# Three of the MLP's four parts of up units in pairs of seven block products, with the input sums made behind the first eight units

## The reference

```python
def sqrelu_mlp(x, w1, w2):        # x 512x1024, w1 1024x4096, w2 4096x1024
    h = jax.nn.relu(x @ w1)
    return (h * h) @ w2

for layer in range(2):
    mix = hybrid_mixer(...) if layer == 0 else recurrent_mixer(...)
    x = layer_norm(DN_ALPHA * x + mix, ...)
    x = layer_norm(DN_ALPHA * x + sqrelu_mlp(x, mlp_w1[layer], mlp_w2[layer]), ...)
```

## Time and profile before

| what | value |
|---|---|
| median of 3 runs | 2314.28 us (2313.63 to 2316.79) |
| the profiled execution's own time | 2314.27 us |
| its span, first to last instruction | 2312.2 us |
| PE busy | 2289.0 us, 99% |
| PE weight load busy | 1954.3 us, 85% |
| DVE busy | 1481.2 us, 64% |
| ACT busy | 1110.8 us, 48% |
| POOL busy | 340.1 us, 15% |
| granted TensorE clock, mean | 1.000 |

### The profile page before, as it was taken

How to read it: one execution, slowest core, us unless ns; L and a number is a source line. 1 busy time by engine, 2 the same in 40 slices (tenths; PEclk the granted TensorE clock), 3 DMA queues, 4 the chain that set the end, 5 groups by cost and what they waited for, 6 DMA issues and landing times.

```text
span 2312.2 us, 33438 instructions
## 1 busy us (share of the span) xinstructions
PE 2289.0 (99%) x13578; PEld 1954.3 (85%) x13578; DVE 1481.2 (64%) x2282; ACT 1110.8 (48%) x1927; POOL 340.1 (15%) x296
## 2 busy tenths in 40 slices
PE   9989999999999999999999999999999999999999
PEld 7768888899988988998978888888888789888887
DVE  6798765456687764555776777636586547775455
ACT  5656453334367543333555654434254556444342
POOL 0041410221321400221420101100010001110000
PEclk9999999999999999999999999999999999999999
DMA  6220222223222232223221232322321113233222
GB/s 212 80 74 2 70 96 75 99 92 127 100 92 92 77 115 81 93 101 127 85 87 58 72 114 96 100 93 94 97 93 55 56 37 110 92 100 98 95 91 64
DMA packets 60601, 207.56 MB, mean 90 GB/s; under 512 B 7024, under 2 KB 9120, under 8 KB 60320
## 3 DMA queue, kind: packets, MB, share of 16 engines
q1 hardware_dynamic: 59536, 202.40, 26.3%
q0 software_dynamic: 640, 2.76, 0.3%
q10 hardware_dynamic: 272, 0.26, 0.0%
HBM read 201.93 MB, written 2.10 MB: 88 GB/s over the span
## 4 chain that ended last, share of the span: by engine, by line
PE 88%; DVE 6%; issue 3%; ACT 2%; POOL 1%; DMA 0%; SPq 0%; DVEq 0%; POOLq 0%
PE ps L331 25%; PE ps L333 24%; PE ps L332 24%; PE ps L1152 2%; PE ps L1151 2%; PE ps L1150 2%; DVE TM L677 1%; PE ps L3242 1%; PE ps L392 1%; PE ps L3213 1%; PE ps L3226 1%; DVE WL L304 1%; PE ps L394 1%; PE ps L393 1%; DVE XL L781 0%
## 5 line engine op out<-in xcount | busy, mean ns | idle before, releaser
L331 PE MATMUL ps<-XH,WH 128*128 128x512 f32 (+1 forms) x1856 | 691.2, 372 | 8.0 <-DVE WL L954 5.6
L333 PE MATMUL ps<-XH,WL 128*128 128x512 f32 (+1 forms) x1856 | 676.0, 364 | 0.0
L332 PE MATMUL ps<-XL,WH 128*128 128x512 f32 (+1 forms) x1856 | 675.9, 364 | 0.0
L304 DVE TENSOR_TENSOR WL<-RAW,WH 128x1024 fp32r<-128x1024 f32 (+2 forms) x409 | 488.0, 1207 | 282.1 <-ACT WH L289 175.8
L289 ACT ACTIVATE WH<-RAW 128x1024 fp32r<-128x1024 f32 (+2 forms) x409 | 411.8, 1020 | 150.5 <-POOL RAW L261 86.8
L331 PE MATMUL ps<-H,WH 128*128 128x512 f32 (+1 forms) x1200 | 431.2, 359 | 0.0
L332 PE MATMUL ps<-H,WH 128*128 128x512 f32 (+1 forms) x1200 | 429.9, 358 | 0.0
L333 PE MATMUL ps<-H,WL 128*128 128x512 f32 (+1 forms) x1200 | 429.5, 358 | 0.0
L331 PEld LDWEIGHTS ps<-XH,WH 128*128 128x128 f32 x1856 | 350.6, 189 | 74.7 <-issue 8.5
L333 PEld LDWEIGHTS ps<-XH,WL 128*128 128x128 f32 x1856 | 350.6, 189 | 56.1
L332 PEld LDWEIGHTS ps<-XL,WH 128*128 128x128 f32 x1856 | 350.8, 189 | 55.1 <-issue 2.2
(11 more groups left out here) (473 smaller groups left out, 3126.1 us busy)
## 6 DMA issues: line engine op xcount, KB each, us to landing
RAW<-in_w SPq DMA_DIRECT2D x128, 512.0 KB, 3.5
RAW<-in_up SPq DMA_DIRECT2D x88, 512.0 KB, 3.5
RAW<-in_dn SPq DMA_DIRECT2D x32, 512.0 KB, 3.4
RAW<-in_hyb SPq DMA_DIRECT2D x20, 512.0 KB, 3.5
RAW<-in_qkv SPq DMA_DIRECT2D x18, 512.0 KB, 3.5
RAW<-in_kvf SPq DMA_DIRECT2D x17, 512.0 KB, 3.5
RAW<-in_rin SPq DMA_DIRECT2D x16, 512.0 KB, 3.4
RAW<-in_dn SPq DMA_DIRECT2D x16, 384.0 KB, 3.0
```

The source lines that it names most:

```text
L304: dve.e.tensor_tensor(WL[:, s, 0:n], RAW[:, s, 0:n], f32(WH[:, s, 0:n]), ALU.subtract).then_inc(*w_lo.at(u))
L331: pe.e.matmul(out, wh, xh, start=first, stop=False)
L332: pe.e.matmul(out, wh, xl, start=False, stop=False)
L333: return pe.e.matmul(out, wl, xh, start=False, stop=last)
```

## The change

Part 1 of the up units moves into the pairs, so that there are twelve pairs in a layer (q = 1, 2, 3) in place of eight, and the down parts 0, 1 and 2 all lie between their products. What is left of plain up units is part 0. All four input sums are now made by DVE behind units m = 1 to 4 of part 0, their low parts behind m = 3, 4, 5 and after m = 7. ACT rounds T1, T2, T4 behind m = 2, 3, 4, and T3 between the relu and the high part of unit m = 7. T3's raw sum has a buffer of its own in AR, so that it no longer waits for the plain up units.

```diff
-PAIRS = [(q, j) for q in (2, 3) for j in range(4)]
+PAIRS = [(q, j) for q in (1, 2, 3) for j in range(4)]
@@ plan_units
-        out = part("w1", 0) + part("w1", 1) + part("w2", 0)
+        out = part("w1", 0)
@@ input sums
-        T_RAW = {... "T3": XF[:, 8:12, LATE]}
+        T_RAW = {... "T3": by256(AR[:, 16:18, :])}
             else:
-                dve.wait_ge(unit_done, UNIT[f"w1_{l}"][15])
+                dve.wait_ge(t_raw, (l, "T4"))
                 a, b = X[:, BACK, LATE], X[:, FRONT, LATE]
@@ mlp_pe
-            for q in range(2):
-                for m in range(8):
-                    if q or m >= 3:
-                        unit(pe, w1[8 * q + m], m % 4, XHS, XLS, ready_of(stage))
-                    pe.until[m % 4] = [(h_sq, (l, q, m))]
             for m in range(8):
-                down(0, m)
+                if m >= 3:
+                    unit(pe, w1[m], m % 4, XHS, XLS, ready_of(stage))
+                pe.until[m % 4] = [(h_sq, (l, 0, m))]
@@ mlp_act
-            for q in range(2):
-                for m in range(8):
-                    p = 8 * q + m - 2
-                    split_for(split_hi, act, w1, 8 * q + m, 3)
-                    act.wait_ge(unit_done, w1[8 * q + m])
-                    ...
-                    high(q, m, TM[:, 4 + m % 2, :])
-                    if q and m in (3, 4, 5):
-                        x_sum_act(act, l, ("T1", "T2", "T4")[m - 3])
             for m in range(8):
-                split_for(split_hi, act, w2, m)
-                if m == 0:
+                split_for(split_hi, act, w1, m, 3)
+                act.wait_ge(unit_done, w1[m])
+                if m > 1:
+                    act.wait_ge(h_sq, (l, 0, m - 2))
+                act.e.activation(TM[:, 2 + m % 2, :], PS[m % 4][:, :], ACT.Relu).then_inc(*h_relu.at((l, 0, m)))
+                if m == 7:
                     x_sum_act(act, l, "T3")
+                high(0, m, TM[:, 4 + m % 2, :])
+                if 2 <= m < 5:
+                    x_sum_act(act, l, ("T1", "T2", "T4")[m - 2])
             split_hi(act, PAIR_AT[l, 0] + 5)
@@ mlp_dve
-            for q in range(2):
-                for m in range(8):
-                    ... (split_lo, square, low)
-                    if q and 1 <= m < 4:
-                        x_sum_dve(dve, l, ("T1", "T2", "T4")[m - 1])
-                    if q and 4 <= m < 7:
-                        x_rest_dve(dve, l, ("T1", "T2", "T4")[m - 4])
-            x_sum_dve(dve, l, "T3")
-            dve.wait_ge(t_raw, (l, "T3"))
             for m in range(8):
-                split_for(split_lo, dve, w2, m)
-                add(0, m)
-                if m == 1:
-                    x_rest_dve(dve, l, "T3")
+                split_for(split_lo, dve, w1, m, 3)
+                ... (square, low)
+                if 1 <= m < 5:
+                    x_sum_dve(dve, l, ("T1", "T2", "T4", "T3")[m - 1])
+                if 3 <= m < 6:
+                    x_rest_dve(dve, l, ("T1", "T2", "T4")[m - 3])
+            x_rest_dve(dve, l, "T3")
             split_lo(dve, PAIR_AT[l, 0] + 5)
```

More of the change, by code:

```diff
@@ L1107, in by256 @@
             return t.rearrange("p a (b t) -> p (a b) t", t=256)
-        T_RAW = {"T1": by256(Y[:, 2:4, :]), "T2": by256(Y[:, 6:8, :]), "T4": by256(TM[:, 6:8, :]), "T3": XF[:, 8:12, LATE]}
+        T_RAW = {"T1": by256(Y[:, 2:4, :]), "T2": by256(Y[:, 6:8, :]), "T4": by256(TM[:, 6:8, :]), "T3": by256(AR[:, 16:18, :])}
         T_HI = {"T1": by256(YR[:, 0:2, :]), "T2": by256(YR[:, 4:6, :]), "T4": by256(TMR[:, 0:2, :]), "T3": XH[:, FRONT, LATE]}
@@ L1222, in high @@
                 act.e.activation(H[:, 16 * (q % 2) + m, :], h, ACT.Copy).then_inc(*h_hi.at((l, q, m)))
-            for q in range(2):
-                for m in range(8):
-                    p = 8 * q + m - 2
-                    split_for(split_hi, act, w1, 8 * q + m, 3)
-                    act.wait_ge(unit_done, w1[8 * q + m])
-                    if p >= 0:
-                        act.wait_ge(h_sq, (l, p // 8, p % 8))
-                    act.e.activation(TM[:, 2 + m % 2, :], PS[m % 4][:, :], ACT.Relu).then_inc(*h_relu.at((l, q, m)))
-                    high(q, m, TM[:, 4 + m % 2, :])
-                    if q and m in (3, 4, 5):
-                        x_sum_act(act, l, ("T1", "T2", "T4")[m - 3])
-            for m in range(8):
-                split_for(split_hi, act, w2, m)
-                if m == 0:
+            for m in range(8):
+                split_for(split_hi, act, w1, m, 3)
[4 more added lines that the diff above has]
+                if m == 7:
                     x_sum_act(act, l, "T3")
+                high(0, m, TM[:, 4 + m % 2, :])
+                if 2 <= m < 5:
+                    x_sum_act(act, l, ("T1", "T2", "T4")[m - 2])
             split_hi(act, PAIR_AT[l, 0] + 5)
@@ L1285, in add @@
                     dve.e.tensor_tensor(X[:, m, :], X[:, m, :], PS[m % 4][:, :], ALU.add).then_inc(*x_mix.at((("mlp", l, q), m)))
-            for q in range(2):
-                for m in range(8):
[L1289 to L1293, removed]
-                    if q and 1 <= m < 4:
-                        x_sum_dve(dve, l, ("T1", "T2", "T4")[m - 1])
-                    if q and 4 <= m < 7:
-                        x_rest_dve(dve, l, ("T1", "T2", "T4")[m - 4])
-            x_sum_dve(dve, l, "T3")
-            dve.wait_ge(t_raw, (l, "T3"))
-            for m in range(8):
-                split_for(split_lo, dve, w2, m)
-                add(0, m)
-                if m == 1:
-                    x_rest_dve(dve, l, "T3")
+            for m in range(8):
+                split_for(split_lo, dve, w1, m, 3)
+                r, h = TM[:, 2 + m % 2, :], TM[:, 4 + m % 2, :]
+                dve.wait_ge(h_relu, (l, 0, m))
+                dve.e.scalar_tensor_tensor(h, PS[m % 4][:, :], 0.0, r, ALU.max, ALU.mult).then_inc(*h_sq.at((l, 0, m)))
+                low(0, m, h)
+                if 1 <= m < 5:
[3 more added lines that the diff above has]
+            x_rest_dve(dve, l, "T3")
             split_lo(dve, PAIR_AT[l, 0] + 5)
```

## The result

The changed kernel takes **2318.99 us** (median of 20 runs, 2317.66 to 2320.55) where the kernel before takes 2314.76 (20 runs, 2313.61 to 2316.79). The ratio is 1.0018 with a 95% interval of 1.0012 to 1.0025: 4.2 us or 0.18% slower. That is just inside the 0.2% taken as the bound, and 2.2 us above the forecast of 2316.8.

A forecast was written before the change was run, and what follows sets the result against it. PE was taken as the bound, busy 99% of the span. From 2314.27 us, less 6.08 saved, plus 8.6 of waiting, came 2316.8 us, called the same within 0.2%; the range was 2309.8 to 2321.3.

The forecast's parts named there:

- The saving, 6.08 us: PE in the MLP: four pair stages of 21.00 us replace 87.04 us of plain work, saving 3.04 a layer.
- Later pairs free: Pairs after the first: their added sums, splits and copies fall where engines idle, costing nothing; stages stay 21.00 us.
- The turns, 3.4 us: Before the first pair, POOL's weight sums and DVE's two-input operations block each other at SBUF, delaying DVE 3.4 us.
- the walk: Forecast's step-by-step timing of DVE's and ACT's in-order lists before layer 0's first pair, using start-to-start distances.
- The wait, 4.3 us a layer: PE in each layer's first pair waits for late DVE and ACT work: 4.3 us a layer, 8.6 in all.
- Square 7: DVE's square of unit m = 7, last of part 0 in layer 0, expected to start at 337.3.
- U2: PE product in the first pair, needing ACT's copy of M1; expected at 340.9 in place of 336.6.
- M5's part: First-pair product M5 needs the low part of unit `two`; expected 1.0 us late, within the 4.3 us wait.
- The clock: Rival, chance 0.22: PE's first-pair rest drops its clock, costing 2.2 us a layer; 2321.2 us if in both layers.

The follow-up runs named there:

- The run with both orders: Changed kernel, with VectorE's input sums between square and low part, and ScalarE's first-pair copies of M1 and M5 ahead of three splits: 2308.34 us, ratio 0.9972.
- the fills: Changed kernel, with GpSimd writing zeros in place of the weight sums in the first pair of each layer: 2309.82 us, ratio 0.9979.
- the filled run: Changed kernel, with 24 extra PE matmuls of 256 columns, read by nobody, before U2 in each layer's first pair: 2315.80 us, ratio 1.0006.
- the run with early sums: Kernel before, pairs unchanged, with T1, T2 and T4 made, rounded and split behind the units of part 0: 2314.96 us, ratio 0.9999.

## Why the prediction was right, and where it was not

- **The saving, 6.08 us.** Right. The run with both orders keeps it whole, and in the changed kernel the POOL sums of later pairs are still 21.0 apart.
- **Later pairs free.** Right. The only waits of PE in either MLP are those of the first pair.
- **The turns, 3.4 us.** Right in kind and nearly in size: the three VectorE rows hold 1.09 + 0.98 + 1.09 = 3.2, at the very operations that the walk named, and the fills gave 3.2 back.
- **The wait, 4.3 us a layer.** Measured 3.84. Square 7 and U2 stand where the walk has them (337.3 and 340.9), but this execution entered the MLP 0.45 later, so that the chain was 0.4 shorter than the walk, 0.2 of it in the turns. M5's part was 0.7 and not 1.0.
- **The clock.** Here the forecast chose wrong. It was a rival with 0.22, and it happened in both layers of the profiled execution. Its place and cause were as named, its size was not: 2.2 us a layer were taken from matmuls of 512 columns at the start of the kernel, where eleven ran slowly (from 6.18 to 10.72 is 4.54 us, which is 2.0 above eleven at 0.227). Here it was 1.5 by the timeline and 1.6 by the filled run. The rival's time would be 2316.8 + 3.0 = 2319.8 with the right size, and with the wait as measured 2314.76 - 6.08 + 7.68 + 2.98 = 2319.3 against 2318.99 measured. So the forecast's miss of 2.2 us is the clock, 3.0, less 0.9 of overpriced waiting, plus 0.5 since the kernel before has a median of 2314.76 over 20 runs and not 2314.27. That makes 2.6, and 0.4 stays unexplained.
- **Range and direction.** The time lies in 2309.8 to 2321.3, and 0.18% is within what was called the same, though 20 runs tell it from no change. That it stayed within is partly luck, since the errors have opposite signs: with the wait as large as forecast, 8.6, and the clock as measured, the time would be 0.9 us longer, 2319.9, where 0.2% ends at 2319.4.

## What to carry to other kernels

Before replacing work by cheaper work, look at what lay between its last use and the next stage: here the 87 us of plain units were the cover under which two engines got ready, and 3 us saved cost 5 in each layer. When a stage needs one small result early, give it its place in the engine's list by when it is needed: moving one copy past two splits and a few sums into a gap of 0.7 us turned 0.18% slower into 0.28% faster. Walk the in-order lists by hand with start-to-start distances. Here such a walk over 27 us of two engines' steps came within 0.5 us.

## What the runs showed of the hardware

The granted clock fell after a rest of 2.9 us that followed another of 0.5 some 3 us before, in both layers. It stayed up with single rests of 1.6 us (PE's wait at line 2144 in the kernel before), of 1.3, of 1.0 and less, and with the rest filled. A fall cost 1.5 us. Rests alone do not tell where it falls. In the run with early sums the clock fell at 165, far ahead of the edit, behind rests of 0.8 and 1.0 us (stretches as above). In the kernel before the same stretch has the same rests and keeps 1.00. This fall cost nothing that can be seen, since PE's next wait for VectorE shrank from 1.6 to 0.3 us:

```profile
163.00:165.00 2.00, 0.68 (x16) 0.55 (x16) 1.86 (x9) 1.13 (x3) 0.00 (x0) 1.00 0.00 0
165.00:168.00 3.00, 2.69 (x17) 2.10 (x18) 2.92 (x7) 1.26 (x6) 0.00 (x0) 0.55 0.00 0
```

The Trainium skill, "SBUF — State Buffer", section "Who interferes with whom", limits the contention of a VectorE instruction with two SBUF inputs to GpSimd instructions that read SBUF. The fills, which only write, agree in the one row that runs beside them: 1.22 for the split, against 2.31 beside the sums.
